# Down projections of four FFNs: six of 22 inner tiles conventionally, the other sixteen by seven block products for each pair of outputs

## The reference, cut to what matters

```python
def swiglu_2(x, w_gate, w_up, w_down):
    return (jax.nn.silu(x @ w_gate) * (x @ w_up)) @ w_down

# first block, FFN 0 and FFN 1
h = h + 0.5 * rmsnorm(swiglu(rmsnorm(h, gn[0]), ffn_w_in[i, 0], ffn_w_out[i, 0]), gn[1])
...
h = h + 0.5 * rmsnorm(swiglu(rmsnorm(h, gn[4]), ffn_w_in[i, 1], ffn_w_out[i, 1]), gn[5])
# second block, FFN 2 and FFN 3
h = h + 0.5 * swiglu_2(rms_norm(h, ffn1_norm[l]), ffn1_w_gate[l], ffn1_w_up[l], ffn1_w_down[l])
...
h = h + 0.5 * swiglu_2(rms_norm(h, ffn2_norm[l]), ffn2_w_gate[l], ffn2_w_up[l], ffn2_w_down[l])
```

## Time and profile before

| | us |
|---|---|
| median of 3 runs | 1989.1 |
| the runs | 1988.85 to 1992.79 |
| span of the profiled execution | 1987.4 |
| PE busy | 1942.5 |
| DVE busy | 1224.5 |
| ACT busy | 946.7 |
| POOL busy | 920.9 |

### The profile page before, as it was taken

How to read it: one execution, slowest core, us unless ns; L and a number is a source line. 1 busy time by engine, 2 the same in 40 slices (tenths; PEclk the granted TensorE clock), 3 DMA queues, 4 the chain that set the end, 5 groups by cost and what they waited for, 6 DMA issues and landing times.

```text
span 1987.4 us, 36265 instructions
## 1 busy us (share of the span) xinstructions
PE 1942.5 (98%) x13268; PEld 1743.7 (88%) x13268; DVE 1224.5 (62%) x1709; ACT 946.7 (48%) x1632; POOL 920.9 (46%) x533
## 2 busy tenths in 40 slices
PE   8999999999999999999999999999999999999999
PEld 8999999997779899988889998887775678999888
DVE  5977660485456877770388778117756548877711
ACT  5566642435324566652356666325336345666522
POOL 3455464543325455555545556544441044555552
PEclk9999999999999999999999999999999999999999
DMA  6233343222412233333223333333311022333331
GB/s 175 64 106 106 94 117 90 73 57 64 114 55 66 75 112 103 106 102 106 85 64 106 106 106 109 102 99 98 80 53 44 1 85 75 106 106 106 107 101 58
DMA packets 344591, 177.89 MB, mean 90 GB/s; under 512 B 18715, under 2 KB 340118, under 8 KB 344494
## 3 DMA queue, kind: packets, MB, share of 16 engines
q1 hardware_dynamic: 342640, 175.46, 30.7%
q10 hardware_dynamic: 1854, 1.07, 0.2%
HBM read 174.42 MB, written 2.10 MB: 89 GB/s over the span
## 4 chain that ended last, share of the span: by engine, by line
PE 85%; DVE 8%; ACT 3%; issue 2%; POOL 1%; DMA 0%; DVEq 0%; ACTq 0%
PE ps L2446 43%; PE ps L2724 35%; DVE xop L1532 1%; DVE hid_r L1616 1%; PE ps L3238 1%; POOL wlo L484 1%; PE ps L3220 1%; PE ps L3197 1%; DVE xop_f L1506 1%; POOL hT L501 1%; DVE xlo L1804 1%; DVE sqbuf L1462 1%; ACT xhi L885 1%; ACT sqbuf L905 0%; PE ps L3201 0%
## 5 line engine op out<-in xcount | busy, mean ns | idle before, releaser
L484 POOL TENSOR_TENSOR wlo<-raw,whi 128x1024 fp32r<-128x1024 f32 x190 | 482.7, 2551 | 605.2 <-ACT whi L610 594.5
L2724 PE MATMUL ps<-xop,whi 128*128 128x256 f32 (+1 forms) x4032 | 724.8, 283 | 14.0 <-ACT wa L756 7.8
L2724 PEld LDWEIGHTS ps<-xop,whi 128*128 128x128 f32 x4032 | 622.6, 190 | 16.5 <-POOL wlo L543 8.5
L2724 PE MATMUL ps<-xop,wlo 128*128 128x256 f32 (+1 forms) x2016 | 568.2, 282 | 0.0
L543 POOL TENSOR_TENSOR wlo<-raw,whi 128x512 fp32r<-128x512 f32 x212 | 289.2, 1368 | 219.3 <-ACT whi L738 219.3
L2724 PEld LDWEIGHTS ps<-xop,wlo 128*128 128x128 f32 x2016 | 381.5, 189 | 0.0
L2446 PE MATMUL ps<-xop,whi 128*128 128x512 f32 (+3 forms) x1176 | 335.4, 343 | 1.9 <-DVE hid_r L1616 1.9
L2446 PE MATMUL ps<-xop,wlo 128*128 128x512 f32 (+3 forms) x924 | 291.3, 342 | 0.0
L610 ACT ACTIVATE whi<-raw 128x1024 fp32r<-128x1024 f32 x176 | 183.1, 1053 | 207.7 <-PE ps L2446 198.8
L738 ACT ACTIVATE whi<-stage 128x512 fp32r<-128x512 f32 x216 | 136.4, 632 | 220.2 <-DVE stage L1556 133.8
L2446 PEld LDWEIGHTS ps<-xop,whi 128*128 128x128 f32 x1176 | 202.7, 188 | 31.1 <-DVE hid_r L1616 3.2
(11 more groups left out here) (399 smaller groups left out, 2792.0 us busy)
## 6 DMA issues: line engine op xcount, KB each, us to landing
raw<-in_ffn_w_in SPq DMA_DIRECT2D x88, 512.0 KB, 3.8
raw<-in_ffn_w_gate SPq DMA_DIRECT2D x44, 512.0 KB, 3.7
raw<-in_ffn_w_up SPq DMA_DIRECT2D x44, 512.0 KB, 3.7
raw<-in_ffn_w_out SPq DMA_DIRECT2D x32, 512.0 KB, 3.9
raw<-in_ffn_w_down SPq DMA_DIRECT2D x32, 512.0 KB, 3.8
raw<-in_a_w_in SPq DMA_DIRECT2D x24, 512.0 KB, 3.8
raw<-in_w_in SPq DMA_DIRECT2D x19, 512.0 KB, 3.8
raw<-in_ffn_w_out SPq DMA_DIRECT2D x16, 384.0 KB, 3.5
```

What stands on the lines that cost most here:

```text
L484: pool.tensor_tensor(wlo[:, u % SLOTS, :], raw[:, u % SLOTS, :], whi[:, u % SLOTS, :].bitcast(F32), ALU.subtract).then_inc(lo_done, 1)
L2724: ins = pe.matmul(ps[:, bank_, 0:h], w[l][:, k * P:(k + 1) * P], x[r][:, k * h:(k + 1) * h], start=start and k == 0 and q == 0, stop=k == ...
```

## The change

Of the 22 inner tiles, six stay conventional: 8 weight units of 768 columns, 6 x 3 matmuls for each output, kept in `ybuf` (FFN 0 and 1, copied by ACT) or added to `hT` (FFN 2 and 3, by DVE). The other sixteen are a left and a right half of eight tiles. For each pair of outputs, the 2 x 2 grid of weights (two outputs by two halves) and the 2 x 2 grid of activations (two halves by two halves of the columns) are multiplied by seven products of 8 tiles x 3 matmuls of half the columns. DVE makes the sums S1 to S4 of 1024 columns for each pair. The sums of the activations T1 to T4 (in two parts, 1024 columns each) are made by DVE once, and ACT, DVE and POOL split B11, B21, B22 and T1 to T4 into hi and lo. After the products DVE adds PSUM into `ybuf` or `hT` (`post`: k1, k5, u2, c22, k23, c21). Three kinds of additions are waited for by PE, since later products add onto the same bank.

The gains of the norm behind FFN 0 and 1 move from L1724 into the transition; the factor 0.5 goes into the square root's scale. The last pair has another order (M1, M2, M6, M4, M7, M5, M3), in which the first half of the columns is complete after M7; the sums for the root and its spreading are put among M5's matmuls. The first weights of the next stage wait for the last pair's blocks instead of a unit's lo (`block_read`).

```diff
-HID_IN_XLO = 6
 NFAST = KF - NCONV
+PAIRS = KD // 2
+DOWN_CONV = 6
+DOWN_HALF = (KF - DOWN_CONV) // 2
+HID_TILES = KF + 2
 
 SLOTS = 4
 UNIT = 1024
 STARTED = 1
-SPLIT = {0: 1, 1: 3, 2: 1}
+SPLIT = {1: 3}
+MIX_OUT = (1, 4)
 LAG = 3
 APART = P // 4
...
+        for d in range(PAIRS):
+            for block in BLOCKS:
+                u = block_unit(i, d, block)
+                if d == 0:
+                    sp.wait_ge(lo_done, u - SLOTS + 1)
+                else:
+                    block_read(sp, i, d - 1, block)
+                m, k0 = OUT_PAIR[d][block in ("A21", "A22")], DOWN_CONV + DOWN_HALF * (block in ("A12", "A22"))
+                sp.dma_start(slot_view(raw, u, DOWN_HALF, P), kcols(f["down"], m * P, P, k0, DOWN_HALF)) \
+                  .then_inc(raw_loaded[u % SLOTS], 16)
...
+    def block_read(sp, i, d, block):
+
+        if block == "A11":
+            sp.wait_ge(*down_sum(i, d, "S2"))
+            sp.wait_ge(*down_sum(i, d, "S3"))
+            sp.wait_ge(*down_lo(i, d, "A11"))
+        if block == "A21":
+            sp.wait_ge(*down_sum(i, d, "S1"))
+            sp.wait_ge(*down_sum(i, d, "S3"))
+        if block == "A12":
+            sp.wait_ge(*down_sum(i, d, "S4"))
+            sp.wait_ge(*down_lo(i, d, "S4" if d == PAIRS - 1 else "A12"))
+        if block == "A22":
+            sp.wait_ge(*down_sum(i, d, "S1"))
+            sp.wait_ge(*down_lo(i, d, "A22"))
...
+        for j in range(5):
+            unit(j)
+        x_lo("B11", 0)
+        unit(5)
+        x_lo("B11", 1)
+        unit(6)
+        unit(7)
+        x_lo("B21", 0)
+        x_lo("B21", 1)
+        lo(0, "A11")
+        lo(0, "A12")
+        lo(0, "S3")
+        x_lo("B22", 0)
+        lo(0, "A22")
+        for d in (1, 2):
+            lo(d, "A11")
+            lo(d, "A12")
+            lo(d, "S3")
+            lo(d, "A22")
+        lo(3, "A11")
+        lo(3, "A12")
+        lo(3, "A22")
+        lo(3, "S3")
...
+        act_down_unit(act, i, 2)
+        act_down_unit(act, i, 3)
+        x_hi("T1", 0)
+        x_hi("T1", 1)
+        keep(0)
+        act_down_unit(act, i, 4)
+        x_hi("B11", 0)
+        x_hi("B11", 1)
+        keep(1)
+        act_down_unit(act, i, 5)
+        x_hi("T2", 0)
+        x_hi("T2", 1)
+        keep(2)
+        act_down_unit(act, i, 6)
+        x_hi("B21", 0)
+        x_hi("B21", 1)
+        keep(3)
+        act_down_unit(act, i, 7)
+        keep(4)
+        hi(0, "A11")
+        keep(5)
+        hi(0, "S1")
+        keep(6)
+        hi(0, "S2")
+        keep(7)
+        hi(0, "A12")
+        x_hi("T3", 0)
+        x_hi("T3", 1)
+        hi(0, "S3")
+        x_hi("B22", 0)
+        x_hi("B22", 1)
+        hi(0, "S4")
+        hi(0, "A22")
+        x_hi("T4", 0)
+        x_hi("T4", 1)
+        for d in (1, 2):
+            hi(d, "A11")
+            hi(d, "S1")
+            hi(d, "A12")
+            hi(d, "S2")
+            square(d - 1)
+            normed(d - 1)
+            hi(d, "S3")
+            hi(d, "S4")
+            hi(d, "A22")
+        hi(3, "A11")
+        hi(3, "A12")
+        hi(3, "S2")
+        hi(3, "A22")
+        square(2)
+        hi(3, "S3")
+        normed(2)
+        hi(3, "S1")
+        hi(3, "S4")
+        cursor[0] = u0 + NU_DOWN
...
+    OUT_PAIR = [(0, 1), (2, 3), (4, 5), (7, 6)]
+    PRODUCTS = [["M1", "M5", "M6", "M2", "M7", "M3", "M4"]] * 3 + [["M1", "M2", "M6", "M4", "M7", "M5", "M3"]]
+    BLOCK_OF = dict(M1="A11", M5="S1", M6="S2", M2="A12", M7="S3", M3="S4", M4="A22")
+    X_OF = dict(M1="B11", M5="T1", M6="T2", M2="B21", M7="T3", M3="B22", M4="T4")
+    D_SUMS = [["S1", "S2", "S3", "S4"]] * 3 + [["S1", "S2", "S4", "S3"]]
+    D_HI = [["A11", "S1", "S2", "A12", "S3", "S4", "A22"]] + [["A11", "S1", "A12", "S2", "S3", "S4", "A22"]] * 2 \
+        + [["A11", "A12", "S2", "A22", "S3", "S1", "S4"]]
+    D_LO_DVE = [["S1", "S2", "S4"]] * 3 + [["S2", "S1", "S4"]]
+    LO_POOL = [("B11", 0), ("B11", 1), ("B21", 0), ("B21", 1), ("A11", 0), ("A12", 0), ("S3", 0), ("B22", 0), ("A22", 0)]
+    LO_POOL += [(block, d) for d in (1, 2) for block in ("A11", "A12", "S3", "A22")]
+    LO_POOL += [(block, 3) for block in ("A11", "A12", "A22", "S3")]
+    D_POSTS = [["k1", "k5", "u2", "c22", "k23", "c21"]] * 3 + [["k1", "k2", "u2", "k4", "c21", "c22", "k5", "u4", "c12"]]
...
                 hid_lo(0, 1)
+                dve_x_sum(v, i, "T1", 0)
             if not first:
                 hidden(prev)
             if not last:
                 s2(nxt)
             else:
                 hid_lo(1, 3)
+                dve_x_sum(v, i, "T1", 1)
             gate(st)
...
+        x_sum("T2", 0)
+        x_sum("T2", 1)
+        out(0)
+        x_sum("T3", 0)
+        x_sum("T3", 1)
+        x_sum("T4", 0)
+        x_sum("T4", 1)
+        out(1)
+        x_lo("T1", 0)
+        x_lo("T1", 1)
+        out(2)
+        x_lo("T2", 0)
+        x_lo("T2", 1)
+        out(3)
+        out(4)
+        s1(0)
+        lo(0, "S1")
+        out(5)
+        s2(0)
+        out(6)
+        lo(0, "S2")
+        out(7)
+        for d in range(3):
+            a, b, c = down_banks(d)
+            if d == 0:
+                x_lo("T3", 0)
+                x_lo("T3", 1)
+            post(d, "k1", "M1", 0, 0, a)
+            s3(d)
+            if d == 0:
+                x_lo("B22", 1)
+            else:
+                squares(d - 1)
+            post(d, "k5", "M5", 1, 1, c)
+            s4(d)
+            if d > 0:
+                gained(d - 1)
+            lo(d, "S4")
+            post(d, "u2", "M6", 0, 1, a)
+            if d == 0:
+                x_lo("T4", 0)
+                x_lo("T4", 1)
+            post(d, "c22", "M7", 1, 1, a, "k5")
+            s1(d + 1)
+            post(d, "k23", "M3", 0, None, b, "u2")
+            if d < 2:
+                lo(d + 1, "S1")
+                s2(d + 1)
+            else:
+                s2(3)
+                s4(3)
+            post(d, "c21", "M4", 1, 0, a)
+            lo(d + 1, "S2")
+        a, b, c, e, f = last_banks(n)
+        post(3, "k1", "M1", 0, 0, a)
+        s3(3)
+        post(3, "k2", "M2", 0, 0, b, "k1")
+        squares(2)
+        lo(3, "S1")
+        post(3, "u2", "M6", 0, 1, a)
+        gained(2)
+        lo(3, "S4")
+        post(3, "k4", "M4", 1, 0, e)
+        if i == 2:
+            for k in range(4):
+                lo_of_x(v, 4, k, n, "mix_norm_2", 0)
+        post(3, "c21", "M7", 1, 0, a, "k4")
+        post(3, "c22", "M7", 1, 1, a)
...
+        def multiply(d, name, bank_, start, between=None):
+            block, x = BLOCK_OF[name], X_OF[name]
+            pe.wait_ge(*down_lo(i, d, block))
+            weights = [down_operand(buf, i, d, block) for buf in (whi, wlo)]
+            for k in range(DOWN_HALF):
+                if d == 0 and k % 4 == 0:
+                    pe.wait_ge(*x_lo_made(i, x, k // 4))
+                if between is not None:
+                    between(k)
+                parts = [x_hi_part(x, k // 4, n), x_lo_part(x, k // 4, n)]
+                for q, (l, r) in enumerate(((0, 0), (0, 1), (1, 0))):
+                    ins = pe.matmul(ps[:, bank_, 0:h], weights[l][:, k * P:(k + 1) * P], parts[r][:, k % 4, :],
+                                    start=start and k == 0 and q == 0, stop=k == DOWN_HALF - 1 and q == 2,
+                                    skip_group_check=True)
+            return ins
+
+        for d in range(3):
+            a, b, c = down_banks(d)
+            if d == 0:
+                pe.wait_ge(s["kept"], down_at[i]["kept"] + KD - 1)
+            elif d == 1:
+                pe.wait_ge(s["kept"], down_at[i]["kept"] + KD)
+            else:
+                pe.wait_ge(*down_post(i, 0, "c21"))
+            multiply(d, "M1", a, True).then_inc(s["mult"], 1)
+            multiply(d, "M5", c, True).then_inc(s["mult"], 1)
+            pe.wait_ge(*down_post(i, d, "k1"))
+            multiply(d, "M6", a, False).then_inc(s["mult"], 1)
+            multiply(d, "M2", b, True).then_inc(s["mult"], 1)
+            pe.wait_ge(*down_post(i, d, "u2"))
+            multiply(d, "M7", a, False).then_inc(s["mult"], 1)
+            pe.wait_ge(*down_post(i, d, "k5"))
+            multiply(d, "M3", c, False).then_inc(s["mult"], 1)
+            pe.wait_ge(*down_post(i, d, "c22"))
+            multiply(d, "M4", a, False).then_inc(s["mult"], 1)
+        a, b, c, e, f = last_banks(n)
+
+        def in_m5(k):
+            if i in (0, 1) and k == 3:
+                sum_down_half(pe, i, 0)
+            if i in (0, 1) and k == 7:
+                spread_half(pe, R0 if i == 0 else R2, 0)
+            if i == 3:
+                final_m5(pe, k)
+
+        def in_m3(k):
+            if i == 3:
+                final_m3(pe, k)
+
+        pe.wait_ge(*down_post(i, 1, "c21"))
+        multiply(3, "M1", a, True).then_inc(s["mult"], 1)
+        multiply(3, "M2", b, True).then_inc(s["mult"], 1)
+        pe.wait_ge(*down_post(i, 3, "k1"))
+        multiply(3, "M6", a, False).then_inc(s["mult"], 1)
+        pe.wait_ge(*down_post(i, 2, "c21"))
```

(6 more changed lines are left out.)

837 lines of the change are left out of this document (569 added, 268 removed).

## The result

The changed kernel takes 2019.7 us (median; 2016.4 to 2023.1) against 1990.9 us before on the same chip (1988.9 to 1996.4): ratio 1.0143, 95% interval 1.0127 to 1.016. It is 29 us slower; the forecast was 21 slower, 2010, with a range up to 2030. The profiled execution's span is 2018.5 us, 31.1 more than the 1987.4 of the earlier trace rows.

The account below looks back on a forecast made before the run. It took TensorE to bound the kernel, time being the number of matmuls times their distance. Terms: -36 matmul work, +3 entry, +52 first-pair waits, +2 clock, sum +21 us, giving 2010 us, range 1972 to 2030.

Parts of the forecast that it names:

- the sign that it had set for itself: First pairs: waits ahead of M6 and M7 absent or below 9 us per FFN would mean the prediction is wrong.
- rival (b): First pair: S1 in time, but x_lo of T3 and B22 blocked; 1982 to 1996 us, chance 0.14.
- Matmul work taken away, 36: Down stages: fewer wide matmuls, more narrow ones at 118.5 ns; 36 us less TensorE work over four FFNs.
- Entering, +0.8 each: Entry to the down stage: hid_lo wait goes, but T1 sums delay the last M4; +0.8 us per FFN, +3 total.
- VectorE and GpSimd exclude each other: Conventional outputs: operations with all inputs in SBUF alternate, a pair costing the sum; VectorE's S1 ends at 36.9 us.
- Where TensorE waits for it: First pair: M6 waits 7.5 us, M7 4.3, M4 1.3; 13 us per FFN, +52 over four.
- TensorE ends the outputs at 34.6: Conventional outputs: TensorE finishes them 34.6 us behind the last M4, before VectorE's S1 ends at 36.9.
- Pairs two to four, 0: Later pairs of 19.9 us: VectorE and GpSimd have room; costed at nothing, up to 1 us each if slack is gone.
- The clock, +2: Down stages: clock dips after the longer new waits; +0.5 us per FFN, +2 in all, at most +8.
- Rival (a): Conventional outputs: alternation does not decide, only the first pair's 3.5 us floor is left; -23 us, 1966, chance 0.2.

Follow-up runs that it names:

- e10_psum: Changed kernel with queues reordered, GpSimd's units first, and in FFN 1 to 3 sums T1 and T2 written into PSUM: ratio 0.9939, 1976.1 us.
- e7_best: Changed kernel, all instructions and values kept, with VectorE's, ScalarE's and GpSimd's queues reordered in entry, conventional outputs and first pair: ratio 1.0036.
- e5_pool_xlo: Changed kernel with the four x_lo of B11 and B21 off GpSimd, copied by ScalarE, subtraction left out (low parts wrong): ratio 0.9991.
- e2_outs: Changed kernel with only VectorE's out(1) to out(4) one place earlier in its queue, in FFN 2 and 3: ratio 1.0133.
- e8_best_xlo: e7_best with the four x_lo of B11 and B21 copied by ScalarE instead of made on GpSimd, subtraction left out: ratio 0.9917, 1974.9 us.
- e13_fill_guard: Changed kernel with nearly all new waits filled by unused matmuls, and GpSimd's first unit behind FFN 0 waiting for VectorE's squares: ratio 1.0123, 2016.1 us.

## Why the prediction was right, and where it was not

The forecast and the measured change by FFN, from the start of one up stage to the next (in FFN 3 to the end):

| FFN | forecast | measured |
|---|---|---|
| 0 | +5.6 | +1.5 |
| 1 | +7.1 | +6.6 |
| 2 | +4.4 | +11.2 |
| 3 | +4.1 | +11.2 |
| sum | +21 | +30.5, and 0.5 ahead of FFN 0 |

By the sign that it had set for itself, the prediction does worse than by its number: waits ahead of M6 and M7 of less than 9 us per FFN were to mean that it is wrong. They are 4.4, 6.2, 4.6 and 4.6 us; with those ahead of M1 and in the outputs they are 7.2, 9.6, 11.8 and 12.1. The cause was right and so were the times at which VectorE delivers; where TensorE stands in the meantime was not. That the total still came within 10 us is in part luck: 4 us too much in FFN 0 against 7 too little in each of FFN 2 and 3. (The upper end of rival (b) adds up to 1994, not 1996; nothing rests on it.)

**Matmul work taken away, 36: right.** 24 narrow matmuls take 2.83 to 2.84 us in the later pairs, 118 ns each; where nothing holds it up (e10_psum) the outputs take 34.3 of the expected 33.6 and 0.6, and two middle pairs of the changed kernel took 39.7 (2 x 19.9).

**Entering, +0.8 each: right in size for FFN 1 to 3, wrong in place.** The up stages got longer by 1.5, 1.2, 0.9 and 1.0. The wait for hid_lo that I had going away stayed (0.6); the one ahead of the last M4 grew from 0.56 to 1.4 to 1.6 in FFN 1 to 3. e7_best, with T1 behind the last hidden, has 0.56. In FFN 0 that wait stayed at 0.57, and the 1.5 us are something else: 3.4 us at the lower clock from 74.0, behind a wait of 1.95 us that the kernel before has too, without the lower clock.

**VectorE and GpSimd exclude each other: right, and decisive.** S1 of the first pair was to end 36.9 behind the last M4; it ends at 897.10 in FFN 1, which is 36.3. k1 was to be at 47.8 and u2 10.0 later: k1 ended at 47.5 and u2 9.9 later (908.30 and 918.24). VectorE's operations take 3.4 us, as named. e5_pool_xlo and e10_psum show that this is the cause and not only a sign.

**Where TensorE waits for it: half right.** Of the 7.5 us ahead of M6 in FFN 0 and 1, 2.7 and 3.4 fell ahead of M1, since ScalarE's keep of output 6 stands behind the high part of S1, which waits for VectorE. I had not followed ScalarE's queue to its waits. M6 waited 2.1 and 2.2 more, M7 2.3 and 4.0 (forecast 4.3), M4 not at all. In FFN 1 the second pair begins 68.6 us behind the last M4; the forecast's 34.6 + 19.9 + 13 is 67.5. The nearness is partly chance: the waits ahead of M1, M6 and M7 are 9.6 and not 13, and the pair, 19.9 + 6.2 of waits, still took 30.7, with 10.2 us at the lower clock.

**FFN 2 and 3: the step that failed.** "TensorE ends the outputs at 34.6" holds where ScalarE keeps them. In FFN 2 and 3 VectorE adds each output into `hT`, in the same queue as the sums that GpSimd holds up, and three banks turn: output 4 waited 5.3 for out(1) and output 7 another 2.0 to 2.2. Eight additions of 0.68 are 5.4 us that the sum of VectorE's work left out; putting some of them earlier (e2_outs) gave back 2.3 and 4.9 us up to the second pair. The outputs took 44.2 and 45.7, the second pair began 71.3 and 72.9 behind the last M4: 4 to 5 late. The rest of the 7 lies further on; in FFN 2 the mixer behind it has two stretches of 3.4 us at the lower clock (from 1367.7 and 1507.6) that it had not before.

**FFN 0:** 4 less than forecast, though the second pair begins 68.4 us behind the last M4, where the forecast had 35.1 + 20.5 + 13 = 68.6. What is missing is the wait of 2.6 of the earlier trace rows and the 3.4 us at the lower clock behind it, worth 1.7: both were in the kernel before and are gone by a shift in time, not by what the change does. The lower clock at 74.0 adds 1.7 the other way.

**Pairs two to four, 0: right.** No wait of over 0.6 us there, as long as the first pair is late; in e8_best_xlo and e10_psum, where it is early, they cost 5 to 7 us in all.

**The clock, +2: about 4 for the part that was taken away, within its bound of 8.** The Trainium skill, TensorE: Matmul & The Clock Gate, section "HAM oscillation — how this bites in real kernels", prices time at the lower clock at half its length; an estimate by it is 29.8 us for the 59.5 added here, and 19.2 for the 38.5 that e13_fill_guard takes away. By that rule the trace does not agree: the time fell by about 4 us. Most of it lay where TensorE would have waited for VectorE a little later: of the changed kernel's 72.6 us, the 6.9 in FFN 2's outputs cost nothing, and M6 of FFN 1 starts 9.7 us behind M1 with the stretch from 900.1 or without it.

**Rival (a)** named the right point (alternation), and e10_psum is what it described: GpSimd and VectorE no longer in each other's way. It gained 12 to 15 us on before and not its 23, since the first pairs still cost 3 to 7 over their ideal and the later pairs some more.

## What to carry to other kernels

Work that is moved to "idle" VectorE and GpSimd must be added up as one engine's work wherever both read SBUF with two inputs; a temporary in PSUM takes an operation out of that sum (23 to 26 us here, and 41 to 44 with a new order of the queues). When the sum does not fit the stretch, reordering moves the waits about; here it gave at most about half of what both gave together (e7_best, 21 to 24 us). Time at the lower clock need not be a cost: fill the wait ahead of it, and see whether the next stage begins earlier.

## What the runs showed that I had not expected

- An operation of VectorE with one input in PSUM and one in SBUF keeps its plain length beside GpSimd, whether it writes SBUF or PSUM (1.21 to 1.23 us, above). One that writes PSUM but has two SBUF inputs does not (2.71).
- In the changed kernel's down stages the waits of 2.1 to 3.4 us were followed by 3.4 us of the lower clock (that of 2.20 in FFN 1 by none). At those of 4.0 to 5.3 it lasted 6.8 us and began 1.2 to 2.0 us before the wait ended (at one of 5.3 it lasted 3.4). Of the six waits of 1.9 to 2.0 us in the whole run three had 3.4 us of it.
- A 6.4 us difference in a stage that no edit touched (288 or 294.8 us behind FFN 0) came from two GpSimd operations that met VectorE's last additions; one wait on GpSimd removed it. Only the profiled executions show it; that of e5_pool_xlo was the slowest of its ten (1996.7 against a median of 1988.5). Comparisons of a few us between kernels of this kind have to be read by stages.
